# A norm handed over token tile by token tile, and modulation blocks moved to GpSimd and into the attention stages

## What is computed

```python
for i in range(DEPTH):                      # DEPTH = 4, kinds sb, moba, swa, sb
    mod = c_act @ ada_w[i] + ada_b[i]
    sh1, sc1, g1, sh2, sc2, g2 = [m[:, None, :] for m in jnp.split(mod, 6, axis=-1)]
    h = modulate(rms_norm(x, norm_gain[i, 0]), sh1, sc1)
    y = attention(h, ...)                   # stick-breaking, MoBA or sliding window
    x = x + g1 * y
    h = modulate(rms_norm(x, norm_gain[i, 1]), sh2, sc2)
    x = x + g2 * swiglu(h, ffn_w_gate[i], ffn_w_up[i], ffn_w_down[i])
x = trunk_layer(x, ctx, c_2, c_ctx_2, w_ada_2, ...)   # "LAT": modulated by c_2, and by c_ctx_2 for the context
```

## Time and profile before

| what | value |
|---|---|
| median of 3 runs (2432.83 to 2444.14) | 2442.58 us |
| the profiled execution | 2443.3 us, of it span 2441.5 us |
| PE busy | 1987.2 us (81%) |
| DVE busy | 1402.3 us (57%) |
| ACT busy | 956.5 us (39%) |
| POOL busy | 108.6 us (4%) |
| mean granted TensorE clock | 0.902 |

### The profile page before, as it was taken

How to read it: one execution, slowest core, us unless ns; L and a number is a source line. 1 busy time by engine, 2 the same in 40 slices (tenths; PEclk the granted TensorE clock), 3 DMA queues, 4 the chain that set the end, 5 groups by cost and what they waited for, 6 DMA issues and landing times.

```text
span 2441.5 us, 34110 instructions
## 1 busy us (share of the span) xinstructions
PE 1987.2 (81%) x14354; PEld 1608.0 (66%) x14354; DVE 1402.3 (57%) x1415; ACT 956.5 (39%) x1353; POOL 108.6 (4%) x135
## 2 busy tenths in 40 slices
PE   3887999765699984679989869996878878767998
PEld 2665787554578763468767657875666677765787
DVE  5774768655466564366644578574335663445554
ACT  3454443333444342344445534334223411224543
POOL 1000000101000011000000000001000112000000
PEclk9998999887799987689999979897879898978999
DMA  7653879542288662167753347683113100023553
GB/s 279 251 212 113 276 251 331 192 174 69 69 269 279 208 222 75 52 203 259 246 172 121 114 161 248 216 317 137 54 52 104 35 4 3 17 86 109 173 189 104
DMA packets 215117, 393.42 MB, mean 161 GB/s; under 512 B 11306, under 2 KB 130102, under 8 KB 199606
## 3 DMA queue, kind: packets, MB, share of 16 engines
q1 hardware_dynamic: 214453, 391.12, 46.9%
q0 software_dynamic: 512, 0.13, 0.0%
HBM read 390.17 MB, written 1.05 MB: 160 GB/s over the span
## 4 chain that ended last, share of the span: by engine, by line
PE 62%; DVE 18%; ACT 11%; issue 6%; DMA 2%; POOL 1%; DVEq 0%; SPq 0%; ACTq 0%
PE G L1878 15%; PE G L1879 15%; PE G L1880 15%; DVE w_lo L1311 6%; ACT w_hi L856 4%; DVE acc L1327 4%; PE A L1924 2%; PE A L2336 2%; PE A L1916 1%; PE A L1896 1%; ACT z_sb L966 1%; PE A L2113 1%; PE G L2350 1%; PE A L1984 1%; POOL e_sb L741 1%
## 5 line engine op out<-in xcount | busy, mean ns | idle before, releaser
L1311 DVE TENSOR_TENSOR w_lo<-raw,w_hi 128x2048 fp32r<-128x2048 f32 (+1 forms) x256 | 569.8, 2226 | 515.6 <-ACT w_hi L856 510.8
L856 ACT CAST w_hi<-raw 128x2048 fp32r<-128x2048 f32 (+1 forms) x256 | 475.2, 1856 | 688.9 <-PE G L1880 590.7
L1878 PE MATMUL G<-w_hi,h_hi 128*128 128x512 f32 (+1 forms) x1376 | 559.8, 407 | 90.0 <-DVE w_lo L1311 47.9
L1879 PE MATMUL G<-w_lo,h_hi 128*128 128x512 f32 (+1 forms) x1376 | 546.9, 397 | 0.0
L1880 PE MATMUL G<-w_hi,h_lo 128*128 128x512 f32 (+1 forms) x1376 | 545.4, 396 | 0.0
L1878 PEld LDWEIGHTS G<-w_hi,h_hi 128*128 128x128 f32 x1376 | 270.0, 196 | 152.9 <-issue 73.3
L1880 PEld LDWEIGHTS G<-w_hi,h_lo 128*128 128x128 f32 x1376 | 269.4, 196 | 57.1
L1879 PEld LDWEIGHTS G<-w_lo,h_hi 128*128 128x128 f32 x1376 | 270.1, 196 | 52.5 <-issue 0.5
L1878 PE MATMUL G<-w_hi,act_hi 128*128 128x512 f32 (+2 forms) x704 | 282.7, 401 | 20.2 <-DVE act_lo L1346 10.5
L1327 DVE SCALAR_TENSOR_TENSOR acc<-raw,c_col,acc 128x2048 f32<-128x2048 f32 x120 | 281.9, 2349 | 25.1 <-DVE w_lo L1311 12.6
L1879 PE MATMUL G<-w_lo,act_hi 128*128 128x512 f32 (+2 forms) x704 | 278.0, 395 | 0.0
(11 more groups left out here) (350 smaller groups left out, 2052.9 us busy)
## 6 DMA issues: line engine op xcount, KB each, us to landing
raw<-in_ada_w SPq DMA_DIRECT2D x96, 1024.0 KB, 5.1
raw<-in_ffn_w_gate SPq DMA_DIRECT2D x88, 512.0 KB, 3.9
raw<-in_ffn_w_up SPq DMA_DIRECT2D x88, 512.0 KB, 5.0
raw<-in_ffn_w_down SPq DMA_DIRECT2D x40, 1024.0 KB, 5.1
raw<-in_w_mlp SPq DMA_DIRECT2D x32, 1024.0 KB, 5.6
raw<-in_w_ada SPq DMA_DIRECT2D x24, 1024.0 KB, 5.0
raw<-in_w_in SPq DMA_DIRECT2D x18, 1024.0 KB, 5.0
raw<-in_sb_w_in SPq DMA_DIRECT2D x32, 512.0 KB, 4.7
```

The source lines that it names most:

```text
L856: nc.scalar.copy(w_hi[:, u % 2, 0:len(kts), 0:n], raw[:, slot].rearrange("p (k n) -> p k n", k=UNIT_K)[:, 0:len(kts), 0:n])\
L1311: nc.vector.tensor_tensor(w_lo[:, u % 2, 0:len(kts), 0:n], raw[:, slot].rearrange("p (k n) -> p k n", k=UNIT_K)[:, 0:len(kts), 0:n], w_hi[ ...
L1878: nc.tensor.matmul(banks[t][:, 0:n], x_hi[:, kt, ts], w_hi[:, u % 2, i, 0:n], start=st, stop=False)
L1879: nc.tensor.matmul(banks[t][:, 0:n], x_hi[:, kt, ts], w_lo[:, u % 2, i, 0:n], start=False, stop=False)
```

## The change

**Norm by token tile.** `norm` on DVE and ACT takes over the last half of the residual. PE signals `tile_done` after the first token tile of the last unit; DVE then does product, addition, root and scaling for tile 0 and tile 1 in turn. The root's correction is two operations folded into the scaling. PE transposes 4 blocks of tile 0, 4 of tile 1, and then the other 8 by pairs as before; ACT and DVE make the splits in that order, with one conversion of a unit between the second and the third split. The next unit waits per token tile (`ready_at`). The down product is cut in units of 2, 4, 4, 4, 4, 4 blocks of 128 rows, not 4, 4, 4, 4, 4, 2.

**Modulation.** Blocks 1 and 2 of every layer 0 to 3 are added by DVE in that layer's own mixer (16 loads), block 0 of layers 1 to 3 by POOL in the feed-forward before it (8 loads, one in three units), and for LAT block 0 by DVE, blocks 1 and 2 by POOL, all 24 in the feed-forward of layer 3. POOL multiplies in place in the ring slot and then adds. r1 and c12 (c1 and c2 in one) are summed near the end of the mixer, r2 after panel 1 of the feed-forward, c0 of the next layer after unit 8 of `down` (of LAT after panel 7 `up`); c12 and r2 of LAT after the first panel of LAT. A DMA of constants for LAT gets a semaphore of its own.

```diff
+            def accumulate(blocks):
+                for _ in range(KT * blocks):
+                    slot, count, (_, l, n) = k.next_load(loads, "pool")
...
+                    link(nc.gpsimd.tensor_tensor(raw[:, slot], raw[:, slot], c_col[:, c:c + 1].broadcast_to([P, 2 * D]), ALU.mult))
+                    nc.gpsimd.tensor_tensor(acc[:, b % 2], acc[:, b % 2], raw[:, slot], ALU.add).then_inc(acc_pool, 1)
+                    sums[0] += 1
+                    pool.wait_ge(acc_pool, sums[0])
+                    pool.sem_inc(raw_free_pool, 1)
...
         for l in range(DEPTH):
+            slots = 2 * len(qkv_panels(KINDS[l])) + 1
+            for i in range(2 * KT):
+                ADA_MIX[l].setdefault(i * slots // (2 * KT), []).append((l, KT + i))
+            n, first = (KT, 4) if l < DEPTH - 1 else (ADA_U, 2)
+            for i in range(n):
+                unit = first + i * (2 * FF // 256 + 6 - first) // n
+                if unit < 2 * (FF // 256):
+                    ADA_UP[l].setdefault(unit // 2, []).append((l + 1, i))
...
+        def by_pool(l, n):
+            return n >= KT if l == LAT else l > 0 and n < KT
+        SUMS = {(l, ("up", 1)): (l, "r2") for l in range(DEPTH)}
+        SUMS |= {(l, ("down", 8)): (l + 1, "c0") for l in range(DEPTH - 1)}
+        SUMS |= {(DEPTH - 1, ("up", 7)): (LAT, "c0"), (DEPTH - 1, ("down", 2)): (LAT, "r1")}
...
+                if last is not None:
+                    last_residual(0, *last)
+                mean_square(0)
+                if last is not None:
+                    last_residual(1, *last)
+                scale_rows(0)
+                mean_square(1)
+                scale_rows(1)
                 for t in range(NT):
-                    nc.vector.tensor_scalar(n_st[:, t], x[:, t], rms_y[:, t:t + 1], None, ALU.mult).then_inc(n_ready, 1)
-                late()
+                    split(lo[:, 0:KT // 2, t * P:t * P + P], hi[:, 0:KT // 2, t * P:t * P + P])
                 between()
-                for q in range(KT // 2):
+                for q in range(KT // 4, KT // 2):
                     split(lo[:, 2 * q:2 * q + 2], hi[:, 2 * q:2 * q + 2])
...
+            def ready_at(f, h):
+                return (f - 3, f - 2) if h == 0 else (f, f)
```

336 lines of the change are left out of this document (194 added, 142 removed).

## The result

The changed kernel takes 2581.43 us (median of 4 runs, 2577.52 to 2585.61) against 2437.89 us for the kernel before in the same runs: a ratio of 1.059, interval 1.055 to 1.0625. (These are four runs of each; the median of 2442.58 us given before the prediction is of three of them.) It is slower, as forecast; the forecast of 2556 us was 25 us too low, and 2581 lies in its range. The increase was forecast as 113.5 us and is 143.5, so 30 us were missing; the time itself is nearer only because the kernel before took 4.7 us less than in the median that I had started from. The profiled execution has a span of 2583.8 us against 2441.5, so 142.3 us more.

What follows compares the result with a forecast made beforehand. PE was taken to bound the feed-forwards, DVE and ACT by turns the mixers. The terms -37 - 36.5 + 63 + 51 + 73 = +113.5 us on 2443.3, with 0.7 off, gave 2556 us; range 2455 to 2620.

Steps and rivals of the forecast that it cites:

- main case: Whole kernel: POOL and DVE lock each other out, 2556 us; with C and D, 2510 to 2620, chance 0.68.
- Part 1: Gaps between stages: the norm by token tile lets PE start earlier; -37 us, bounds -15 to -60.
- c12 and r2 come behind the first panel, 3.75 + 3.54, with a wait of about 5: Layer 3 to LAT: these sums and PE's wait for ACT's copies offset some 10 us saved; +2 us.
- Part 2: Start of the feed-forwards: waits behind three accumulations ahead of the first act_st, and slower clock, go; -36.5 us.
- Part 3: Mixers: more accumulations in layers 1 to 3, and sums at 6 us each; +63 us, bounds +25 to +90.
- 6 of 8 on the chain, 8 more give 15 us: Layer 2's mixer: most present accumulations are on the chain, so eight more were to add 15 us.
- Part 4 and 5: Feed-forwards of layers 0 to 2: POOL takes 8.4 us a load and holds DVE up; +51 us, bounds 0 and +90.
- Part 6: Layer 3's feed-forward: double accumulations, then 16 POOL loads within 18 units; +73 us, bounds +35 and +95.
- A: Feed-forwards: POOL and DVE hardly disturb each other, or DVE's idle time takes the waits; 2467 or 2493 us, chance 0.17.
- C: Feed-forwards: POOL slower, 9.3 us a load, all collisions of the worse kind; 2609 us, within the shared chance 0.68.
- B: Mixers hide the accumulations as well, POOL costs as in A; 2424 us, chance 0.15 with its neighbourhood.
- D: Gaps: the new norm brings nothing, the second unit waits for the splits; 2578 us, within the shared chance 0.68.

Runs made afterwards that it cites:

- pool_memset: Changed kernel with POOL's product and sum replaced by four zeroings of 128x2048, which read no input; 2474.5 us.
- pool_scalar: Changed kernel with POOL's product as a multiplication of one tile by a per-partition scalar instead of two tensors; 2560.8 us.
- all_dve: Changed kernel with the same order of loads and sums, but DVE adds all blocks and POOL none; 2473.9 us.
- ahead_start: Kernel ahead with the first three loads of each feed-forward put in front of the first act_st again; 2459.2 us.
- ahead: Changed kernel, but DVE adds all 24 next-layer loads in each feed-forward, with r1 and c12 of layers 1 to 3 summed there; 2431.3 us, 0.996 of the kernel before.
- pool_short: Changed kernel with POOL's product and sum on 256 of 2048 columns, loads, order and waits kept; 2460.8 us.

## Why the prediction was right, and where its steps failed

**Sign and size.** Right: the mechanism of the main case holds, POOL and DVE shut each other out by whole instructions. That is no longer read from one pair at a rotation. In the changed kernel 51 instructions `w_lo` of 128x2048 start while POOL's product or sum runs; they take 2.45 to 6.72 us, and each ends 2.1 to 2.2 us behind POOL's end. The 191 others take 2.29 us. The other way round, a product or sum of POOL that starts while `w_lo` runs ends 3.5 or 4.5 us behind DVE's end, its own full time. In pool_memset POOL without inputs leaves `w_lo` at 2.29 us in every place. `act_st`, which reads PSUM, started 31 times beside a POOL operation and took 0.41 to 0.42 us each time. The Trainium skill, "SBUF — State Buffer" (section "SBUF: two separate sides"), has it as an exclusive lock for a DVE instruction with two SBUF inputs, and only against a POOL instruction that reads SBUF. That trace agrees, and pool_memset too; the tail of pool_scalar's product, some 1.5 us in which `w_lo` ran freely, doesn't fit "for the whole instruction", if POOL's recorded end is right. The size is helped by errors of opposite sign: against the forecast the mixers are 18 us, the feed-forwards of layers 0 to 2 20 us and layer 3's 6 us too low, and the way from layer 3 to LAT is 13 us too high. The first reading was too wide as well: PE busy for 197 to 199 us at 0.97 or 0.98 is right for layers 0 to 2 only, in layer 3 it is 207.65 of 224.46 us at 0.93.

**Part 1, the norm: right.** The gaps are 12.47 us behind a mixer and 8.5, 6.9 and 8.5 behind a feed-forward, forecast as 12 to 13 and 8 to 9 (the 6.9 is below that). DVE and PE behind layer 1's mixer (it ended at 670.65), against the earlier trace rows:

```profile
673.97 0.69 DVE L1466 TENSOR_TENSOR n_st<-G,gates 128x512 f32<-128x512 f32 x1
...
678.92 1.09 PE L1992 MATMUL A<-consts,n_st 128*128 128x128 f32 x4 [8.27 <-DVE n_st L1439]
...
683.12 0.77 PE L1974 MATMUL G<-w_hi,h_hi 128*128 128x512 f32 x1
```

One term of it was wrong by 13 us: from layer 3 to LAT I had +2, and it is -11.1, of which -12.3 are the gap (32.6 to 20.3 us), near the 10 that I had put. The step "c12 and r2 come behind the first panel, 3.75 + 3.54, with a wait of about 5" took their whole time as lost. PE at that place:

```profile
1835.44 3.49 PE L2034 MATMUL A<-consts,acc 128*128 128x1 f32 x30
1839.24 3.49 PE L2023 MATMUL A<-acc,consts 128*128 128x512 f32 x4 [0.31 <-issue]
1843.40 0.51 PE L1974 MATMUL G<-w_hi,h_hi 128*128 128x512 f32 x1 [0.68 <-ACT gates L913]
```

The sums take 7.3 us there from first to last, without a wait for more than 0.3. But before, PE waited 5.0 us for `w_lo` behind that place (the next line is from the wait list of the kernel before, 1680.26 to 1757) and 1.7 us for issue; of these 1.8 and 0.3 are left. ACT's copies cost 0.7, not 5. LAT's first window grew by 1.2 us only. That figure is not exact: the same code takes 518.5 us in pool_memset and 527.3 in all_dve.

```profile
PE G L1878 <- DVE w_lo L1311: 5.0, 1, 5.0
```

**Part 2, the start: near in its price, wrong in what stood beside it.** The waits at the start went, as forecast: PE reaches the first transposition of a feed-forward 18.0 or 18.1 us behind its first product in all four layers, before 21.3, 23.1, 21.3 and 29.7. ahead_start has three accumulations ahead of the first `act_st` at 28 to 34 us. The 36.5 counted all seven waits as the start's; three of them, 3.9 us together, lay at later transpositions. The net is smaller than the price: the changed feed-forwards without POOL are only 13.5 us shorter in layers 0 to 2 (617.6 to 604.2 in all_dve's windows), where my terms give about 20. And three things in these stages had no term at all. The sum r2 came in, 1.9 us of PE in each layer. The sums r1 and c1 left, 3.7 us of PE in each. And a new wait stands at the last transposition, which now follows a `down` unit of two blocks where it followed one of four; here in all_dve, 2.64 us in each of layers 0 to 2, where the kernel before waits 0.3 us or not at all:

```profile
354.49 0.66 PE L2217 MATMUL A<-consts,act_st 128*128 128x128 f32 x4 [2.64 <-DVE act_st L1632]
```

No run changed the cut of the down product, so that it causes this wait is read from the order only, and the three don't add up to the missing 6.5 us exactly.

**Part 3, the mixers: mis-sized in layer 2.** Forecast 158, 210, 178 and 158 us, measured 159.8, 215.1, 191.2 and 157.5. The sums are priced right (6 each; 7.5, 5.1 and 7.3 measured), layer 3's 16 accumulations too (18 after the sums; 157.5 - 132.6 - 7.3 = 17.6). In layer 2 the step "6 of 8 on the chain, 8 more give 15 us" failed: they gave 29 us, or 22 by the 184.6 us that the same mixer takes in three other kernels. Against ahead, the eight loads of the kernel before cost 157.0 - 147.8 = 9.2 us, and sixteen cost 191.2 - 147.8 - 5.1 = 38.3 (or 31.7). A share of the chain says what the present loads cost at their present density. I drew a straight line through it, and didn't see that the new places put 14 of them among six units. There DVE's accumulations have 52% of the chain that ended last, and the four-slot ring no longer holds the next unit. In layer 1, with twelve such units, eight more cost 13 us, forecast 10.

**Part 4 and 5, POOL beside DVE: 51 forecast, 64 measured.** The pair's undisturbed price of 8.2 us was 8.4 in the forecast. The step that was too low is "2.5 us for the 18 loads in panels and 1 us for the 6 in `down`": it is 2.7 us for all 24, and the three stages stand at 221 to 225 us where I had named 212. In layer 0 the excess of DVE's operations over their free time is 101.1 - 32 x 2.29 = 27.8 us for `w_lo` and 19.2 - 11 x 0.69 = 11.6 for `act_lo`; 23.6 of these 39 reach the end of the stage.

**Part 6, layer 3: near, with two terms mis-sized.** Forecast about +56 with its share of the start, measured +62.4. POOL makes 47 us (against all_dve) to 51 (against pool_short), and 54 against ahead, whose stage has the same code as all_dve's; forecast 55. The rest of the new order makes 11.6 us net (pool_short, 236.1 against 224.5), where 18 less the start's 17 gives 1. Both terms were off, as these two rows show, PE before at the first transposition and pool_short's window of the four panels with double accumulations:

```profile
1452.85 0.48 PE L2113 MATMUL A<-consts,act_st 128*128 128x128 f32 x1 [11.49 <-DVE act_st L1538]
```

```profile
1460.55:1528.08 67.53, 51.24 (x213) 40.38 (x213) 61.15 (x36) 25.05 (x27) 5.55 (x4) 0.94 0.75 248
```

The wait of 11.49 us went and the way to the first transposition fell from 29.7 to 18.0 us: 11.6 came back, not 17. The four panels take 67.5 us, 21.5 above four times 11.5, not 18.

**Rivals.** A (2467 to 2493) is out: it needed POOL and DVE not to disturb each other, and what it describes is what all_dve and pool_memset take, 2474 us. C had POOL slower and every collision of the worse kind; POOL was not slower (8.2 us), and of the 53 us that it adds to the main case about a quarter was there, the 13 of part 5. B and D are out by the mixers and by the gaps.

## What to carry to other kernels

Before work moves to GpSimd, look at the vector operations that will stand beside it. If the DVE instruction has two inputs in SBUF and the GpSimd instruction reads SBUF too, the two engines take turns, and 8 us of free GpSimd time cost the critical engine some 3. Moving work from a stage bounded by PE, with idle time on DVE, into stages bounded by DVE was a loss here; instead count how many pieces fit between two operations on which PE waits (here one, not two) and how many loads a ring can hold between two units. And price a moved operation at both ends: where it leaves, and where it arrives. Last, look at a stage whose code did not change before you read a difference of a few microseconds in one that did.

## What the runs showed of the hardware

- `w_lo` (two SBUF inputs) that has to wait for a POOL product or sum of 128x2048 ends 2.1 to 2.2 us behind it in all 51 cases of the changed kernel; a POOL operation that has to wait for `w_lo` ends its own full time behind that.
- A product of one tile by a per-partition scalar on POOL takes 5.45 us for 128x2048, longer than the product of two tensors, the second spread from one column (3.60 us). During the last 1.5 us or more of its recorded time a two-input DVE instruction runs freely.
- Zeroing 128x2048 on POOL takes 1.81 us and doesn't disturb DVE at all: 65 us of POOL work in a stage of 201.3 us left no trace in its length.
- In layer 2's first six units the queues moved 351 GB/s with full loads and 169 with short ones, in the same time (45.7 and 45.8 us).
